# Gate and up projections of experts 3 to 16: half of the K-tiles in three passes of split operands, with weights moved in runs of 4096 bytes

## The chip, the cores and the metric

One core of a Trainium2 chip runs the whole program in one launch. The metric is the time on the device in microseconds (us), median of three runs.

## What is computed

Two layers of a transformer block on 512 tokens of 1024 features, all in float32. A layer is a mixer (three kinds of attention, 12 gated projections) and then a mixture of 16 experts, of which each token takes two. The change touches the experts alone:

```python
hid = jax.nn.silu(jnp.einsum('bsd,edf->bsef', h, w_g)) * jnp.einsum('bsd,edf->bsef', h, w_u)
hid = hid * gate[..., None].astype(hid.dtype)
return jnp.einsum('bsef,efd->bsd', hid, w_d)     # d = 1024, f = 256, 16 experts
```

`h` is the normed input (`rms_norm(x, norm_ffn_g[l])`). An expert's weights are 3 MB: 1 MB each for gate, up and down.

## The kernel before

Each engine has its own program, written out by hand, and the engines meet at semaphores. Nothing is scheduled by a tool: the order of the code is the order on the engine.

**The experts, one after the other.** Expert e has up to 128 token slots. GpSimd gathers their normed rows from DRAM into `gather_rows` (two buffers, `gather_tokens`). TensorE turns them in eight transposes into the banks S[0] and S[1] (`turn_gathered`). ScalarE (S[0]) and VectorE (S[1]) copy them into `et`, times the gain of the norm (`et_out`). TensorE multiplies them by the gate and up weights, 8 K-tiles of 128 rows, side by side in one bank of 512 columns (`gate_up`); these are plain float32 matmuls, and the hardware takes two instructions per K-tile. ScalarE takes silu, VectorE the product with up; TensorE turns the result (`turn_hidden`), VectorE splits it into a high and a low part (`hid_hi`, `hid_lo`), and TensorE multiplies by the down weights in three passes of fp32r operands (`down`, by the helper `three`: high by low, low by high, high by high). ScalarE writes the high part of the down weights (`weights_hi`), GpSimd the low part (`weights_lo`). The rows go out times their weight (`rows_down` on ScalarE for one half, VectorE for the other), and GpSimd adds them into DRAM with an indirect DMA (`add_rows`).

**The order on TensorE** for step e of the loop is: `gate_up(e)`, `turn_gathered(e + 1)`, `down(e - 1)`, `turn_hidden(e)`. In this text T(e) is the moment at which `gate_up(e)` ends. ScalarE then does silu(e), `et_out(e + 1)`, `rows_down(e - 1)`, `weights_hi(e)`. VectorE does the product (e), `et_out(e + 1)`, the second half of the rows (e - 1), `hid_hi` and `hid_lo` (e). GpSimd does gather (e + 3), `weights_lo(e)`, `add_rows(e - 1)`. In steps 1 and 2 VectorE also works out the routing of the tokens past 128 of an expert (`route_rows`, `route_blocks`).

**The weights** lie in a ring `work` of six slots of 1 MB, three pieces per expert: K-tiles 0 to 3 of gate and up (piece 0), K-tiles 4 to 7 (piece 1), down (piece 2). SyncE's queue issues them in order, and a slot is loaded again when its old piece is used up:

```python
used, per = ((first_half, 1), (gu_done, 1), (down_lo, 2))[(n - RING) % PIECES]
sp.wait_ge(used, per * ((n - RING) // PIECES + 1))
```

A K-tile takes rows k x 128 to k x 128 + 127 of the matrix, so a partition gets a run of 256 floats, 1024 bytes, from each K-tile, and 4096 bytes from each row of down.

Semaphores that the change and the prediction touch: `gu_done` (gate_up(e) ended), `first_half` (its first four K-tiles ended), `et_act` and `et_dve` (the two halves of `et` written), `hid_done` (product ready), `down_hi` and `down_lo` (parts of the down weights ready), `piece_in` (a slot loaded), `e_hot`, `e_counted`, `e_known` (routing of the tokens past 128).

Of the kernel before, what the change touches and what calls it, by code (L numbers as in the profile page):

```python
# [60 lines left out]
PIECES = 3  # L61

# [116 lines left out]
def hybrid_block(nc, x, rel_bias, norm_mix_g, w_in, qk_norm_g, diff_lambda, diff_subln_g, sinks, w_branch,  # L179
# [24 lines left out]
    with ctx:  # L204
# [67 lines left out]

        wr = sb("wr", [P, KT, 20])
# [82 lines left out]
        pre_eids = sem("pre_eids")  # L356

# [91 lines left out]
        down_lo = sem("down_lo")  # L449
        down_done = sem("down_done")  # L450
# [19 lines left out]
                     down_lo, down_done, y_act, y_dve, x_stored, w_ready, w_counted, w_known]  # L470
# [60 lines left out]
        def _(sp):  # L531
# [83 lines left out]
            parameters(0)  # L615
            sp.dma_start(probs[0:N_BUCKETS, 1, 0:REL_HEADS], rel_bias).then_inc(pre_b, 16)
# [3 lines left out]
            for l in range(DEPTH):  # L620
# [27 lines left out]
                for n in range(PIECES * N_EXPERTS):  # L648
# [30 lines left out]
                def over_weights(i):  # L679
                    e = sp.value_load(over_expert[0:1, i:i + 1], min_val=0, max_val=N_EXPERTS - 1)  # L680
                    le = l * N_EXPERTS + e
                    for part in range(PIECES):
# [8 lines left out]
                        if part < 2:  # L691
                            for half, w in enumerate((w_ff_gate, w_ff_up)):
                                src = w.rearrange("l e d f -> (l e) d f")[bass.ds(le, 1), part * 512:(part + 1) * 512, :]
                                sp.dma_start(work[:, slot, :, half * FF:(half + 1) * FF],
                                             src.rearrange("a (k p) n -> p (a k) n", p=P)).then_inc(piece_in[slot], 16)
# [14 lines left out]
        def _(pool):  # L710
# [27 lines left out]
            for l in range(DEPTH):  # L738
# [117 lines left out]
        def _(pe):  # L856
# [280 lines left out]
            def gate_up(e):  # L1137
                if e:
                    pe.wait_ge(et_act, e + 1)
                    pe.wait_ge(et_dve, e + 1)  # L1140
                if e >= 2:
                    pe.wait_ge(hid_done, e - 1)
                for part in range(2):
                    n = PIECES * e + part
                    pe.wait_ge(piece_in[n % RING], 32 * (n // RING + 1))
                    for kk in range(4):
# [5 lines left out]
                        if e == 0 and kt == 4:  # L1152
                            pe.wait_ge(et_dve, 1)
                        last = nc.tensor.matmul(G[e % 2][:, :], et[:, e % 2, kt * P:(kt + 1) * P],  # L1154
                                                work[:, n % RING, kk, :], start=(kt == 0), stop=(kt == KT - 1))
# [11 lines left out]
            def down(e):  # L1167
# [4 lines left out]
                for c in range(2):  # L1172
                    if e < N_EXPERTS - 1:
                        pe.wait_ge(down_lo, 2 * e + c + 1)
# [14 lines left out]
            for l in range(DEPTH):  # L1189
# [67 lines left out]
                for e in range(N_EXPERTS + 1):  # L1257
# [19 lines left out]
                    if e == 4:  # L1277
# [8 lines left out]
                    if e == 5:  # L1286
# [1016 lines left out]
```

## Time and profile before

| | |
|---|---|
| time, median of 3 runs | 1417.36 us (1416.01 to 1417.49) |
| span of the profiled execution, first to last instruction | 1414.7 us |
| what lies around the span, from the median | 2.7 us |
| TensorE busy | 1380.1 us (98%) |
| VectorE, ScalarE, GpSimd busy | 747.1, 501.9, 762.0 us |
| experts of layer 0 / layer 1 in the span | about 516 to 699 us / 1220 to 1412 us |

The profile is of one execution. Busy time is a sum over instructions; what a second of an engine is worth is read from the chain of work that ended last. SyncE's rows are DMA issues, not transfers.

### The profile page before, as it was taken

To read this page: it belongs to the slowest core of one execution; us is meant where nothing else is said; L and a number is where in the kernel's file an instruction comes from. 1 tells how busy PE (TensorE), PEld (TensorE's weight loads), DVE (VectorE), ACT (ScalarE), POOL (GpSimd) and SP (SyncE) were. 2 spreads that over 40 slices of the span, in tenths; PEclk is the share of its full clock that TensorE was granted. 3 is DMA by queue.
4 is the path that set the end of the run, shared out by engine and by line. 5 is a ranking of instruction groups with operands and counts; after the bars stand their busy time and mean duration, and the time that the engine had idled before them with its cause. 6 is when DMAs were issued, how large, how long until landed. Compare 5 with 4: busy or idle time off the path is not lost.

```text
span 1414.7 us, 19421 instructions
## 1 busy us (share of the span) xinstructions
PE 1380.1 (98%) x6804; PEld 1014.5 (72%) x6804; DVE 747.1 (53%) x1917; ACT 501.9 (35%) x1194; POOL 762.0 (54%) x643
## 2 busy tenths in 40 slices
PE   7999999999999999999889999999999999999997
PEld 5788877777777866656477887777777778665563
DVE  4487856656684155222146787675658543452221
ACT  4322333433432143334243332334343412343331
POOL 4566654454445625676545575544444554266763
PEclk9999999999999999999899999999999999999999
DMA  5435322223312758999732243222322147689995
GB/s 153 127 101 172 118 79 82 74 70 102 88 61 75 278 198 288 322 348 339 197 115 77 69 121 90 80 63 84 84 95 78 61 143 267 234 272 332 329 345 133
DMA packets 148567, 224.26 MB, mean 159 GB/s; under 512 B 18634, under 2 KB 95876, under 8 KB 148462
## 3 DMA queue, kind: packets, MB, share of 16 engines
q1 hardware_dynamic: 136030, 197.59, 43.4%
q0 software_dynamic: 9936, 16.81, 5.0%
q10 hardware_dynamic: 2496, 8.52, 1.5%
q8 instruction: 58, 0.95, 0.3%
q14 instruction: 47, 0.39, 0.1%
HBM read 215.47 MB, written 31.25 MB: 174 GB/s over the span
## 4 chain that ended last, share of the span: by engine, by line
PE 91%; DVE 4%; ACT 1%; issue 1%; POOL 1%; DMA 1%; SPq 0%; POOLq 0%; DVEq 0%; ACTq 0%
PE bank L859 20%; PE bank L861 18%; PE bank L860 18%; PE bank L1154 16%; PE bank L1035 4%; PE bank L1047 3%; PE bank L1068 2%; PE bank L1116 2%; PE bank L988 1%; PE bank L1058 1%; DVE probs L1849 1%; PE bank L1001 1%; POOL w_lo L733 1%; DVE mixed L1666 1%; PE bank L1126 1%
## 5 line engine op out<-in xcount | busy, mean ns | idle before, releaser
L727 POOL TENSOR_SCALAR w_hi<-raw 128x1024 fp32r<-128x1024 f32 (+2 forms) x142 | 148.7, 1047 | 418.1 <-PE bank L861 415.3
L733 POOL TENSOR_TENSOR w_lo<-raw,w_hi 128x512 fp32r<-128x512 f32 (+2 forms) x288 | 359.1, 1267 | 16.4 <-ACT w_hi L1579 4.6
L860 PE MATMUL bank<-w_hi,hT_lo 128*128 128x512 f32 (+2 forms) x696 | 258.5, 371 | 0.0
L1154 PE MATMUL bank<-work,ptmp 128*128 128x512 f32 x512 | 225.5, 592 | 1.0 <-ACT ptmp L1515 1.0
L859 PE MATMUL bank<-w_lo,hT_hi 128*128 128x512 f32 (+2 forms) x576 | 216.2, 375 | 2.4 <-DVE hT_lo L1674 1.0
L861 PE MATMUL bank<-w_hi,hT_hi 128*128 128x512 f32 (+2 forms) x576 | 211.6, 367 | 0.0
L1154 PEld LDWEIGHTS bank<-work,ptmp 128*128 128x128 f32 x512 | 94.6, 190 | 107.6 <-issue 106.2
L795 POOL TENSOR_TENSOR w_lo<-work,w_hi 128x512 fp32r<-128x512 f32 x120 | 148.1, 1263 | 43.0 <-ACT w_hi L1531 43.0
L859 PE MATMUL bank<-hT_lo,w_hi 128*128 128x512 f32 x384 | 159.5, 415 | 0.0
L861 PE MATMUL bank<-hT_hi,w_hi 128*128 128x512 f32 x384 | 150.7, 393 | 0.0
L860 PE MATMUL bank<-hT_hi,w_lo 128*128 128x512 f32 x384 | 150.1, 391 | 0.0
L860 PEld LDWEIGHTS bank<-w_hi,hT_lo 128*128 128x128 f32 x696 | 131.2, 188 | 20.5 <-issue 0.5
L859 PEld LDWEIGHTS bank<-w_lo,hT_hi 128*128 128x128 f32 x576 | 108.4, 188 | 28.8 <-issue 8.5
L861 PEld LDWEIGHTS bank<-w_hi,hT_hi 128*128 128x128 f32 x576 | 108.4, 188 | 17.8
L859 PEld LDWEIGHTS bank<-hT_lo,w_hi 128*128 128x128 f32 x384 | 72.1, 188 | 32.8 <-issue 20.5
L2118 DVE TENSOR_TENSOR sq<-sq,bank 128x256 f32<-128x256 f32 x32 | 13.4, 420 | 150.8 <-ACT sq L1623 150.8
L861 PEld LDWEIGHTS bank<-hT_hi,w_hi 128*128 128x128 f32 x384 | 72.1, 188 | 16.5
L771 POOL DMA_INDIRECT probs<-normed_dram,slot_token x32 | 33.2, 1037 | 89.9 <-PE bank L1116 67.6
L860 PEld LDWEIGHTS bank<-hT_hi,w_lo 128*128 128x128 f32 x384 | 72.4, 188 | 12.5
L859 PE MATMUL bank<-oT_lo,w_hi 128*128 128x512 f32 x192 | 79.4, 413 | 0.5 <-DVE hT_lo L1907 0.5
L1623 ACT ACTIVATE sq<-bank 128x256 f32<-128x256 f32 x32 | 12.3, 384 | 184.4 <-PE bank L1154 184.4
L861 PE MATMUL bank<-oT_hi,w_hi 128*128 128x512 f32 x192 | 76.1, 396 | 0.0
(308 smaller groups left out, 2342.7 us busy)
## 6 DMA issues: line engine op xcount, KB each, us to landing
work<-in_w_ff_gate SPq DMA_DIRECT2D x66, 512.0 KB
work<-in_w_ff_up SPq DMA_DIRECT2D x66, 512.0 KB
work<-in_w_ff_down SPq DMA_DIRECT2D x33, 1024.0 KB, 6.7
raw<-in_w_gate SPq DMA_DIRECT2D x48, 512.0 KB, 3.9
raw<-in_w_in SPq DMA_DIRECT2D x40, 512.0 KB, 3.5
raw<-in_w_branch SPq DMA_DIRECT2D x24, 512.0 KB, 3.6
raw<-in_w_out SPq DMA_DIRECT2D x16, 512.0 KB, 3.7
normed_dram<-mixed ACTq DMA_DIRECT2D x8, 512.0 KB, 2.7
```

The costliest lines, as they stand in the source:

```text
L727: nc.gpsimd.tensor_scalar(w_hi[:, two, :, 0:w], raw[:, slot, :, 0:w], 1.0, 0.0, ALU.mult, ALU.add).then_inc(split_hi, 1)
L733: last = nc.gpsimd.tensor_tensor(w_lo[:, two, kk, 0:w], raw[:, slot, kk, 0:w], w_hi[:, two, kk, 0:w].bitcast(F32), ALU.subtract)
L771: nc.gpsimd.indirect_dma_start(out=gather_rows[:, e % 2, :], out_offset=None, in_=xn_dram, in_offset=bass.IndirectOffsetOnAxis(ap=rows, ax ...
L795: last = nc.gpsimd.tensor_tensor(w_lo[:, c, f, :], rows[:, f, c * 512:(c + 1) * 512], w_hi[:, c, f, :].bitcast(F32), ALU.subtract)
L859: nc.tensor.matmul(out_ap, s_hi, m_lo, start=start, stop=False)
L860: nc.tensor.matmul(out_ap, s_lo, m_hi, start=False, stop=False)
L861: return nc.tensor.matmul(out_ap, s_hi, m_hi, start=False, stop=stop)
L1035: last = nc.tensor.matmul(S[m][:, cols], q[r, job.u, job.i * P:(job.i + 1) * P], k[r, keys], start=True, stop=True)
L1047: last = nc.tensor.transpose(T[0][:, col:col + P], prob_bufs[job.g % 3][:, mm, b * P:(b + 1) * P], ident[:, :])
L1068: last = nc.tensor.matmul(O[HD * m:HD * (m + 1), job.i * P:(job.i + 1) * P], v, p[:, m, b * P:(b + 1) * P], start=(b == 0), stop=(b == len ...
L1116: last = nc.tensor.transpose(S[a][:, q * P:(q + 1) * P], gather_rows[:, e % 2, dt * P:(dt + 1) * P], ident[:, :])
L1154: last = nc.tensor.matmul(G[e % 2][:, :], et[:, e % 2, kt * P:(kt + 1) * P], work[:, n % RING, kk, :], start=(kt == 0), stop=(kt == KT - 1))
```

## The change

For experts 2 to 15 (the third to the sixteenth; `splits(e)`), in each of the two layers, K-tiles 4 to 7 of `gate_up` are taken in three passes of fp32r parts in place of float32 matmuls. The gathered half in S[1] is copied to `et_hi` by ScalarE without the gain, and VectorE subtracts to get `et_lo`. The gain goes to the weights: ScalarE writes `gu_hi` (weights times gain, four instructions of 128x512), VectorE `gu_lo` (the rest), both two experts ahead of their use. The low part of the second half of the down weights moves from GpSimd to VectorE (`down_lo_half`). K-tile k of gate and up now takes every fourth row of a half of the matrix, so that a partition's four rows are one run of 4096 bytes; the gathered rows are written in the same order of features, and the gains are loaded in it (`ffn_gain`, two small loads at the start). `route_blocks` is cut in two, for steps 2 and 3, and what TensorE, VectorE and the waits do with it comes one step later. Experts 0, 1 and the blocks past 128 tokens keep float32, in the new order.

```diff
+FIRST_SPLIT = 2
+def split_count(e):
+    return 4 * (e - FIRST_SPLIT + 1)
...
+        et_hi, et_lo = hT_hi[:, 0:2, :], hT_hi[:, 2:4, :]
+        gu_hi_bufs = [[oT_hi[:, k, :] for k in range(4)], [hT_lo[:, k, :] for k in range(4)]]
+        gu_lo_bufs = [[oT_lo[:, k, :] for k in range(4)], [hT_hi[:, 5, :], hT_hi[:, 6, :], hT_hi[:, 7, :], hT_lo[:, 6, :]]]
+        def splits(e):
+            return FIRST_SPLIT <= e < N_EXPERTS
+        def in_expert_order(rows):
+            return rows.rearrange("p (a n k) -> p a k n", a=2, k=4)
+        def gate_up_piece(slot):
+            return work[:, slot].rearrange("p k n -> p (k n)").rearrange("p (h k n) -> p h k n", h=2, k=4)
...
+            for m in range(DEPTH):
+                sp.dma_start(ffn_gain[:, m, :].rearrange("p (a k) -> p a k", k=4),
+                             layer_of(norm_ffn_g, m).rearrange("l (a p k) -> p (l a) k", a=2, k=4)
+                             ).then_inc(gains_in, 16)
...
-                        used, per = ((first_half, 1), (gu_done, 1), (down_lo, 2))[(n - RING) % PIECES]
-                        sp.wait_ge(used, per * ((n - RING) // PIECES + 1))
+                        old = (n - RING) // PIECES
+                        if part == 0:
+                            sp.wait_ge(first_half, old + 1)
+                        elif part == 1 and splits(old):
+                            sp.wait_ge(gu_lo, split_count(old))
+                        elif part == 1:
+                            sp.wait_ge(gu_done, old + 1)
+                        else:
+                            sp.wait_ge(down_lo, old + 2)
+                            if old:
+                                sp.wait_ge(down_lo_dve, old)
...
-                            sp.dma_start(work[:, slot, :, half * FF:(half + 1) * FF],
-                                         src.rearrange("a (k p) n -> p (a k) n", p=P)).then_inc(piece_in[slot], 16)
+                            sp.dma_start(gate_up_piece(slot)[:, half],
+                                         src.rearrange("a (p k) n -> p (a k) n", p=P)).then_inc(piece_in[slot], 16)
...
-                    for c in range(2):
+                    for c in range(1 if e else 2):
                         pool.wait_ge(down_hi, 2 * e + c + 1)
...
+                    if part and splits(e):
+                        pe.wait_ge(et_dve, e + 1)
+                        for kk in range(4):
+                            pe.wait_ge(gu_lo, split_count(e - 1) + kk + 1)
+                            rows = slice(kk * P, (kk + 1) * P)
+                            last = three(G[e % 2][:, :], et_hi[:, e % 2, rows], et_lo[:, e % 2, rows],
+                                         gu_hi_bufs[e % 2][kk], gu_lo_bufs[e % 2][kk], False, kk == 3)
+                        last.then_inc(gu_done, 1)
+                        continue
...
+                if splits(e):
+                    act.wait_ge(et_turned, 2 * e + 2)
+                    nc.scalar.activation(et_hi[:, e % 2, :], S[1][:, :], ACT.Copy).then_inc(et_hi_done, 1)
+            def gate_up_hi(e):
+                n = PIECES * e + 1
+                act.wait_ge(piece_in[n % RING], 32 * (n // RING + 1))
+                for kk in range(4):
+                    nc.scalar.activation(gu_hi_bufs[e % 2][kk].rearrange("p (h n) -> p h n", h=2),
+                                         gate_up_piece(n % RING)[:, :, kk, :], ACT.Copy,
+                                         scale=ffn_gain[:, l, 4 + kk:5 + kk]).then_inc(gu_hi, 1)
...
                     if 1 <= e < N_EXPERTS - 1:
                         weights_hi(e)
+                    if splits(e + 2):
+                        gate_up_hi(e + 2)
...
+                if splits(e):
+                    v.wait_ge(et_hi_done, e - FIRST_SPLIT + 1)
+                    nc.vector.tensor_tensor(et_lo[:, e % 2, :], S[1][:, :], et_hi[:, e % 2, :].bitcast(F32),
+                                            ALU.subtract).then_inc(et_dve, 1)
+                    return
...
+            def gate_up_lo(e):
+                n = PIECES * e + 1
+                for kk in range(4):
+                    v.wait_ge(gu_hi, split_count(e - 1) + kk + 1)
+                    nc.vector.scalar_tensor_tensor(gu_lo_bufs[e % 2][kk].rearrange("p (h n) -> p h n", h=2),
+                                                   gate_up_piece(n % RING)[:, :, kk, :], ffn_gain[:, l, 4 + kk:5 + kk],
+                                                   gu_hi_bufs[e % 2][kk].bitcast(F32).rearrange("p (h n) -> p h n", h=2),
+                                                   ALU.mult, ALU.subtract).then_inc(gu_lo, 1)
+            def down_lo_half(e):
+                v.wait_ge(down_hi, 2 * e + 2)
+                nc.vector.tensor_tensor(w_lo[:, 1, :, :], down_rows(e)[:, :, 512:1024], w_hi[:, 1, :, :].bitcast(F32),
+                                        ALU.subtract).then_inc(down_lo_dve, 1)
...
+                    if 1 <= e < N_EXPERTS - 1:
+                        down_lo_half(e)
...
+                    if splits(e + 2):
+                        gate_up_lo(e + 2)
+                    if e in (2, 3):
+                        route_blocks(e - 2)
```

On TensorE, from the end of step 1 to step 2 of layer 0, before: the turn of the hidden rows (`sq`), `gate_up` (`work` by `ptmp`, where `et` lies), the turn of the gathered rows (`probs`), and the first K-tile of `down`:

```order
L1163 MATMUL bank<-ident,sq 128x128 x2
L1154 MATMUL bank<-work,ptmp 128x512 x8
L1116 MATMUL bank<-ident,probs 128x128 x8
L859 MATMUL bank<-w_lo,hT_lo 128x512
L860 MATMUL bank<-w_hi,hT_lo 128x512
L861 MATMUL bank<-w_hi,hT_lo 128x512
```

The same place in the changed kernel (`gu_hi` and `gu_lo` of an even expert lie in `oT_hi` and `oT_lo`):

```order
L1215 MATMUL bank<-ident,sq 128x128 x2
L1205 MATMUL bank<-work,ptmp 128x512 x4
L900 MATMUL bank<-oT_lo,hT_hi 128x512
L901 MATMUL bank<-oT_hi,hT_hi 128x512
L902 MATMUL bank<-oT_hi,hT_hi 128x512
...
L1157 MATMUL bank<-ident,probs 128x128 x8
L900 MATMUL bank<-w_lo,hT_lo 128x512
```

Four of the eight K-tiles stay float32, and the other four are three matmuls each (12 rows, of which three are shown).

On ScalarE, one step before: silu, `et_out`, `rows_down`, `weights_hi`, and the silu of the next step:

```order
L1623 ACTIVATE sq<-bank 128x256
L1515 ACTIVATE ptmp<-bank,pcol 128x128 x4
L1540 ACTIVATE mixed<-bank,slot_weight 128x512
L1531 ACTIVATE w_hi<-work 128x1024 x2
L1623 ACTIVATE sq<-bank 128x256
```

And of the change, where `gu_hi` lies in `oT_hi` or in `hT_lo`:

```order
L1693 ACTIVATE sq<-bank 128x256
L1570 ACTIVATE ptmp<-bank,ffn_gain 128x128 x4
L1581 ACTIVATE hT_hi<-bank 128x512
L1607 ACTIVATE mixed<-bank,slot_weight 128x512
L1598 ACTIVATE w_hi<-work 128x1024 x2
L1588 ACTIVATE oT_hi<-work,ffn_gain 128x512 x4
L1693 ACTIVATE sq<-bank 128x256
```

Five instructions per step are new: `et_hi` (L1581), which stands ahead of `rows_down`, and the four of `gate_up_hi` (L1588), which stand ahead of the next silu.

On VectorE, step 2 of the change: product, `et_lo`, rows, `hid_hi`, `hid_lo`, then what is new, `down_lo_half` (L2200), `gate_up_lo` (L2192) and the first half of `route_blocks` (L2161 on), and the product of step 3:

```order
L2215 TENSOR_TENSOR sq<-sq,bank 128x256
L2179 TENSOR_TENSOR hT_hi<-bank,hT_hi 128x512
L2225 TENSOR_SCALAR mixed<-bank,slot_weight 128x512
L2235 CAST hT_lo<-bank 128x256
L2237 TENSOR_TENSOR hT_lo<-bank,hT_lo 128x256
L2200 TENSOR_TENSOR w_lo<-work,w_hi 128x1024
L2192 SCALAR_TENSOR_TENSOR oT_lo<-work,ffn_gain,oT_hi 128x512 x4
L2161 SCALAR_TENSOR_TENSOR raw<-raw,rank 128x8
L2164 TENSOR_SCALAR raw<-o_rows,raw 128x128 x4
...
L2215 TENSOR_TENSOR sq<-sq,bank 128x256
```

The product of the next step, on which TensorE's next `turn_hidden` waits, now stands behind `gate_up_lo`.

## Rows read from the trace of the kernel before

**Rows 1.** The page's slices: granted clock and DMA share, each over 1/40 span.

```profile
PEclk9999999999999999999899999999999999999999
DMA  5435322223312758999732243222322147689995
```

**Rows 2.** The chain that ended last, one expert: start us, us, what.

```profile
608.22 6.87 PE bank L1154 x16
615.08 0.87 PE bank L1116 x8
615.96 0.23 PE bank L859
...
618.49 0.23 PE bank L861
618.72 0.22 PE bank L1163 x2
618.93 6.44 PE bank L1154 x15
```

**Rows 3.** Timeline of the other engines, one expert: start us, us, engine, line.

```profile
604.41 0.38 ACT L1623 ACTIVATE sq<-bank 128x256 f32<-128x256 f32 x1 [5.88 <-PE bank L1154]
604.84 1.14 ACT L1515 ACTIVATE ptmp<-bank,pcol 128x128 f32<-128x128 f32 x4
...
606.67 0.69 ACT L1540 ACTIVATE mixed<-bank,slot_weight 128x512 f32<-128x512 f32 x1 [0.69 <-PE bank L861]
607.26 1.99 ACT L1531 ACTIVATE w_hi<-work 128x1024 fp32r<-128x1024 f32 x2
...
608.39 4.94 POOL L795 TENSOR_TENSOR w_lo<-work,w_hi 128x512 fp32r<-128x512 f32 x4 [1.35 <-ACT w_hi L1531]
...
609.15 0.42 DVE L2140 TENSOR_TENSOR hT_lo<-bank,hT_lo 128x256 fp32r<-128x256 f32 x1
...
613.36 0.37 SPq L667 DMA_DIRECT2D work<-in_w_ff_down  x1
```

**Rows 4.** DMA from 576 to 684 us: share in 40 slices, queues.

```profile
DMA  9999997999999999999999999999999999999998
...
DMA packets 26245, 36.20 MB, mean 335 GB/s; under 512 B 2470, under 2 KB 22406, under 8 KB 26239
...
q1 hardware_dynamic: 23301, 30.89, 83.4%
q0 software_dynamic: 2938, 5.22, 19.5%
```

**Rows 5.** Queue q1, 668 to 670 us, then 594 to 596: packets, MB, share.

```profile
q1 hardware_dynamic: 661, 0.72, 111.9%
...
q1 hardware_dynamic: 195, 0.80, 99.7%
```

**Rows 6.** Groups by form: busy us, mean ns, idle before.

```profile
L1504 ACT ACTIVATE hT_hi<-bank 128x512 fp32r<-128x512 f32 x16 | 9.6, 600 | 39.1 <-DVE bank L1903 39.1
...
L1611 ACT ACTIVATE mixed<-X,row_rs 128x1024 f32<-128x1024 f32 x8 | 9.2, 1152 | 2.7 <-ACT mixed L1611 2.5
...
L1579 ACT ACTIVATE w_hi<-raw 128x512 fp32r<-128x512 f32 x4 | 2.3, 623 | 8.0 <-PE bank L861 8.0
...
L1907 DVE SCALAR_TENSOR_TENSOR hT_lo<-bank,hT_hi 128x512 fp32r<-128x512 f32 x16 | 11.0, 686 | 0.3
```

**Rows 7.** Timeline, steps 1 and 2: GpSimd, VectorE and the SyncE queue.

```profile
542.33 4.94 POOL L795 TENSOR_TENSOR w_lo<-work,w_hi 128x512 fp32r<-128x512 f32 x4 [1.38 <-ACT w_hi L1531]
...
543.66 2.40 DVE L2066 SCALAR_TENSOR_TENSOR raw<-rank,raw 128x8 f32<-128x8 f32 x2
...
547.29 0.37 SPq L667 DMA_DIRECT2D work<-in_w_ff_down  x1
...
554.38 3.89 DVE L2082 TENSOR_SCALAR raw<-o_rows,raw 128x128 f32<-128x128 f32 x4
...
558.29 0.97 DVE L2082 TENSOR_SCALAR raw<-o_rows,raw 128x128 f32<-128x128 f32 x4
```

More of the change, by code:

```diff
@@ L356, in hybrid_block @@
         pre_eids = sem("pre_eids")
+        gains_in = sem("gains_in")
         par = sem("par")
@@ L693, in over_weights @@
                                 src = w.rearrange("l e d f -> (l e) d f")[bass.ds(le, 1), part * 512:(part + 1) * 512, :]
-                                sp.dma_start(work[:, slot, :, half * FF:(half + 1) * FF],
-                                             src.rearrange("a (k p) n -> p (a k) n", p=P)).then_inc(piece_in[slot], 16)
+                                sp.dma_start(gate_up_piece(slot)[:, half],
+                                             src.rearrange("a (p k) n -> p (a k) n", p=P)).then_inc(piece_in[slot], 16)
                         else:
@@ L1139, in gate_up @@
                     pe.wait_ge(et_act, e + 1)
+                if e and not splits(e):
                     pe.wait_ge(et_dve, e + 1)
@@ L1154, in gate_up @@
                         last = nc.tensor.matmul(G[e % 2][:, :], et[:, e % 2, kt * P:(kt + 1) * P],
-                                                work[:, n % RING, kk, :], start=(kt == 0), stop=(kt == KT - 1))
+                                                gate_up_piece(n % RING)[:, :, kk, :], start=(kt == 0),
+                                                stop=(kt == KT - 1))
                     last.then_inc(first_half if part == 0 else gu_done, 1)
@@ L1172, in down @@
                 for c in range(2):
-                    if e < N_EXPERTS - 1:
-                        pe.wait_ge(down_lo, 2 * e + c + 1)
+                    if e < N_EXPERTS - 1 and (c == 0 or e == 0):
+                        pe.wait_ge(down_lo, e + 2 if e else c + 1)
+                    elif e < N_EXPERTS - 1:
+                        pe.wait_ge(down_lo_dve, e)
                     if e >= 1:
@@ L1311, in over_block @@
                             last = nc.tensor.matmul(G[0][:, :], et[:, 0, kt * P:(kt + 1) * P],
-                                                    work[:, n % RING, kk, :], start=(kt == 0), stop=(kt == KT - 1))
+                                                    gate_up_piece(n % RING)[:, :, kk, :], start=(kt == 0),
+                                                    stop=(kt == KT - 1))
                     last.then_inc(e_gu, 1)
@@ L2074, in route_rows, with route_blocks @@
                 link(nc.vector.tensor_reduce(listed, a_cmp[:, :, :, :], AX.X, ALU.add))
-            def route_blocks():
-                block, later, listed = (a_calc[:, n] for n in range(3))
+            def route_blocks(half):
+                block, later, listed, late_weight = (a_calc[:, n] for n in range(4))
+                for t in range(TT) if half else ():
+                    nc.vector.tensor_scalar(over_onehot[:, 1, t, :], slot_id, block_rank[:, 1, t:t + 1], None,
+                                            ALU.is_equal)
+                if half:
+                    for k in range(2):
+                        link(nc.vector.tensor_tensor(over_token[:, k, :, 8:16], over_token[:, k, :, 0:8],
+                                                     late_weight[:, k].unsqueeze(2).broadcast_to([P, TT, 8]), ALU.mult))
+                        last = nc.vector.tensor_tensor(over_token[:, k, :, 0:8], over_token[:, k, :, 0:8],
+                                                       later[:, k].unsqueeze(2).broadcast_to([P, TT, 8]), ALU.mult)
+                    last.then_inc(e_hot, 1)
+                    return
@@ L2078, in route_blocks @@
                 link(nc.vector.scalar_tensor_tensor(block_rank[:, :, :], block, -float(CAPACITY), rank[:, :, :],
                                                     ALU.mult, ALU.add))
+                for t in range(TT):
+                    nc.vector.tensor_scalar(over_onehot[:, 0, t, :], slot_id, block_rank[:, 0, t:t + 1], None,
+                                            ALU.is_equal)
                 for k in range(2):
-                    for t in range(TT):
-                        nc.vector.tensor_scalar(over_onehot[:, k, t, :], slot_id, block_rank[:, k, t:t + 1], None,
-                                                ALU.is_equal)
@@ L2087, in route_blocks @@
                 link(nc.vector.scalar_tensor_tensor(later, block, 0.5, tokens[:, :].unsqueeze(1).broadcast_to([P, 2, TT]),
                                                     ALU.is_gt, ALU.mult))
-                late_weight = a_calc[:, 3]
                 link(nc.vector.scalar_tensor_tensor(late_weight, block, 0.5, weight[:, :, :], ALU.is_gt, ALU.mult))
-                for k in range(2):
-                    link(nc.vector.tensor_tensor(over_token[:, k, :, 8:16], over_token[:, k, :, 0:8],
-                                                 late_weight[:, k].unsqueeze(2).broadcast_to([P, TT, 8]), ALU.mult))
-                    last = nc.vector.tensor_tensor(over_token[:, k, :, 0:8], over_token[:, k, :, 0:8],
-                                                   later[:, k].unsqueeze(2).broadcast_to([P, TT, 8]), ALU.mult)
@@ L2096, in route_blocks @@
-                last.then_inc(e_hot, 1)
             def et_out(e):
```

35 lines of the change are left out of this document (21 added, 14 removed).

## The prediction

> **What bounds the kernel now.** I read the table of busy times first: TensorE is busy 98% of the span, every other engine about half. The slices show its clock at full rate almost throughout, and the DMA line standing out in two stretches, 6 to 10 tenths against 2 to 4 elsewhere: those are the experts [rows 1]. Then the chain of work that ended last, through one expert. It is TensorE without a gap: `gate_up` 6.87 us, eight transposes 0.87, twelve three-pass matmuls of `down` (one each 0.23) and two transposes to 618.93, so 10.71 us from one `gate_up` to the next [rows 2]. Third, the timeline of the others in such a period. With T the end of `gate_up` (604.37, one period before 615.08), silu starts at T+0.04, the four copies of `et` end at T+1.6, `weights_hi` ends at T+4.9, VectorE's `hid_lo` at T+5.2, GpSimd's `weights_lo` at T+9.0, and SyncE's queue sends the next pieces at T+9.0 [rows 3]. None holds TensorE. Last the DMA: from 576 to 684 us no slice is under 7 tenths, the two queues together are at 103% (packets in flight overlap), and 36.20 MB in 108 us are 3.59 MB per expert [rows 4]. So two resources are full: TensorE, on the chain, and the DMA, not on it, but with no room.
>
> **TensorE's part.** A float32 K-tile costs 6.87/8 = 0.859 us, and there are four of them: 3.435. A three-pass K-tile costs what one of `down` costs: (618.72 - 615.96)/4 = 0.69, four are 2.76, entry from the transposes included [rows 2]. Saved: 0.675 an expert, which I round to 0.67 for switching kinds of operand inside a bank, a step that no row shows alone. 14 experts x 2 layers x 0.67 = **18.8 us**. The period becomes 10.05. Below this, 0.58 would be 16.2 in all, if the switch costs the 0.09 that separates the first pass from the others at its worst. The clock, already at the 2.4 GHz level, can't add anything [rows 1].
>
> **ScalarE's part.** `et_hi`, a plain copy from a bank, is priced 0.60 [rows 6]. The four of `gate_up_hi` read SBUF: 0.62 without a scale, and a scale from SBUF adds a tenth (1.15 for 1024 columns with it, about 1.05 as in 1.99 for two without [rows 3, 6]); back to back I take 0.65 each, 2.6. ScalarE's 4.2 of 10.7 become 7.4 of 10.05: it is no bound. But its place in the order matters. `gate_up_hi(e+2)` stands ahead of silu(e+1) and waits for piece 1 of expert e+2, which before was needed only by TensorE almost a period later. How late may it be? From silu's start to the end of `et` are 1.6 us, and `gate_up` starts 3.85 after T (618.93 - 615.08) [rows 2, 3]. So silu may start at T+2.3, and with 2.6 of its own work ahead of it the piece must have landed by **T(e+1) - 0.3**.
>
> **VectorE's part.** Per step `down_lo_half` (1024 columns; 0.686 for 512, so about 1.2) and four of `gate_up_lo` (0.69 each, 2.75) [rows 6]. With the old 2.7 it is 6.7 of 10.05. There is a hold-up: while GpSimd worked on `w_lo` without a break, two VectorE instructions on 8 columns of SBUF took 2.40 us, each waiting for a GpSimd instruction (4.94/4 = 1.24) to end; four of 128 columns took 3.89 against 0.97 for four when GpSimd was done [rows 7]. Now `down_lo_half` at T+5.2 meets GpSimd's two instructions (T+4.0 to T+6.5, then a little later), and `gate_up_lo` begins about T+7.7 and ends near T+10.3, the next product being due at T+10.05+0.45. It just fits. The Trainium skill (GPSIMD Engine Reference, Key points) says the same: GpSimd shares its SBUF interfaces with VectorE, in contention with instructions of two SBUF inputs. By that rule each of the five new VectorE instructions can be held; the trace agrees in 1.2 us a time.
>
> In steps 1 to 3 VectorE also has `route_rows` and the halves of `route_blocks` (four at 0.97 and a handful of 0.2: 2.1 us) behind `gate_up_lo`, ahead of the product [rows 7]. In step 2 `gate_up_lo(4)` can't end before the first long burst has landed (557, below) and 2.6 + 0.65 more: 560; the blocks end at 562.2, the product of step 3 at 562.6, while TensorE wants it at T(3)+3.6 = 562.0. So 0.5 to 1 us is lost here, and perhaps 0.3 in step 3. I take **1 us a layer**, 0 to 2.
>
> GpSimd loses two instructions of 1.24 per expert and gains nothing; the moved routing has a whole step of room; the two gain loads go out in the first 20 us, where TensorE waits for norms. The scaled copies to DRAM stay 1.15 each before TensorE's first expert, now with strided input. All of this: 0, up to +1.
>
> **The DMA's part.** Same bytes, but two of three pieces in packets of 4096 in place of 1024 bytes. Piece 2 already has such packets. A stretch of 661 packets (mean 1.09 KB) moved 0.72 MB in 2 us, one of 195 packets (4.1 KB) 0.80 MB [rows 5]. For 2.10 MB: 5.83 against 5.25 us, **0.58 less** an expert. Since the engines had no gaps I set the DMA's work for an expert at the period, 10.72, so W = 10.14 after; uncertain by 0.3. The Trainium skill (DMA: Bandwidth & Descriptors, Why small descriptors are slow) gives about 3 cycles per packet on top of one per 32 bytes: 35/32 against 131/128, 6.4% less, 0.37 us of 5.83, W = 10.35. The same page puts HBM to SBUF at about 358 GB/s per core, which would make W 3.59/0.358 = 10.03; the row of 0.80 MB in 2 us is above that limit, so I don't use it.
>
> Is it in time? The first steady burst went out at 547.29, behind `weights_lo(1)` [rows 7]. GpSimd now has half (542.33 + 2.5), so 544.8. With 10.14 of transfer and 2 for issue and landing (my allowance) piece 1 of expert 4 lands at 557. The k-th lands at 557 + (k-1)W, and is needed by T(k+2) - 0.3, where T(2) = 549.0 - 0.67 = 548.3, plus 10.05 a step, plus 1.7 from step 5 for the routing matmuls, plus the 1 us lost above. For the last, k = 12: needed by 671.3, landed at 557 + 11W. So **W up to 10.39 costs nothing**, and what is beyond costs 11 x (W - 10.39) a layer. With 10.14 there is nothing; over the range of W I allow 0.3 a layer.
>
> **The sum.** -18.8 + 2 x 1.0 + 2 x 0.3 = -16.2, and +0.3 for the start: -15.9. The profiled execution has a span of 1414.7, 2.7 under the median, so a span of 1398.8 and a time of **1401.5 us**.
>
> **Rivals.**
> - *The DMA becomes the bound* because 4096-byte runs gain little (the 8% between the two rows is from two short stretches, and the shares beside them, 112% and 100%, could be read as more or less). With W = 10.72, 11 x 0.33 = 3.6 a layer: 1401.5 + 7.3 - 0.6 = 1408. With W = 10.9, since the queue was slipping a little already, 5.6 a layer: 1412. For it: the unbroken nines. Against: what is in flight at 103% may not be the limit. Chance 0.27, 1405 to 1413.
> - *Everything hides*: the burst lands by 556, VectorE gets ahead of GpSimd, no loss in steps 2 and 3: 1417.4 - 18.8 = 1398.5. Chance 0.14.
> - *Slower*: larger packets of the weights push the indirect queue aside (gather and scatter share the 16 engines, 19.5% [rows 4]), silu waits for piece 1 in each step, and W rises instead. All gain is gone when 11 x (W - 10.39) = 8, at W = 11.1; at 11.5 it is 12.2 a layer and 1425. The Trainium skill (DMA: Bandwidth & Descriptors, Queues, rings and completion order) says that an engine changes between queues only at a packet's end, which is the mechanism; the trace holds no case of it, both kinds of packet having stood beside the indirect queue in each period. Chance 0.06.
> - *The change buys nothing on TensorE*, a three-pass tile costing what a float32 one does when operands switch: within 0.2% of before. `down` shows 0.69 in the same loop. Chance 0.03.
>
> **The numbers.** Likeliest, 1399.5 to 1405: 0.50. The range 1398 to 1411 takes in most of the first two rivals and leaves some 0.17 out. A difference of 0.2% (2.8 us) is about what a measurement of this kernel tells from none. Faster: 0.50 + 0.14 + 0.26 = 0.90; same 0.04; slower 0.06.
>
> **What would show it.** In the new trace: periods of 10.05 on the chain, `gate_up`'s second half at 2.76; `gate_up_hi` starting at T+7.5 to T+9, its wait put down to the DMA or to nothing; gaps on TensorE only ahead of `turn_hidden` in steps 2 to 4, released by VectorE's product. If instead TensorE waits for `et` (ScalarE) in late steps, and more with each, the DMA is the bound. Wrong altogether: a period over 10.4 from the first steps on.

## The result, and the profile after

Slower: **1434.87 us** (median of 4 runs, 1433.97 to 1438.44) against 1416.93 (4 runs, 1416.01 to 1417.49) on the same chip, a ratio of 1.0133 with the interval [1.0118, 1.0147]. The prediction was 1401.5. The span of the profiled execution is 1433.6, 18.9 more than before.

The DMA share in the slices of the changed kernel's page, to be held against [rows 1]:

```profile
DMA  5436322222213758999632242322322246688894
```

The end of the DMA line, layer 1's experts, reads 46688894 where it read 47689995. The queues in layer 0, 576 to 684 us, which answers to [rows 4]:

```profile
DMA  9969993799999998999189979998899879998999
...
DMA packets 10896, 35.05 MB, mean 325 GB/s; under 512 B 2355, under 2 KB 2355, under 8 KB 10890
...
q1 hardware_dynamic: 8062, 29.89, 73.1%
q0 software_dynamic: 2828, 5.08, 18.7%
```

The share of q1 is 10 points lower, and there are holes in a line that had none under 7. The share has to be read with care: runs_only, below, has 76.0% without a single late step, so most of the fall is the longer packets. What is left is 29.89 MB in the 108 us against 30.89: fewer bytes, and yet the weights are late. The page's line of the chain that ended last, by engine:

```profile
PE 78%; DMA 8%; DVE 5%; ACT 3%; issue 3%; POOL 3%; SPq 1%; ACTq 0%; POOLq 0%; DVEq 0%
```

The chain through experts 7 and 8 of layer 0, whose answer before is the unbroken TensorE of [rows 2]. Columns: start, us, what.

```profile
601.68 2.28 POOL w_lo L836
...
603.98 0.38 SPq L708
...
605.86 13.48 DMA work<-in_w_ff_up
...
619.36 0.73 ACT hT_lo L1588
...
620.12 1.87 DVE hT_hi L2192 x3
...
622.11 0.74 DVE hT_lo L2192
622.86 0.34 DVE sq L2215
...
623.24 0.65 PE bank L1215 x2
623.89 4.92 PE bank L1205 x8
628.81 0.23 PE bank L900
```

GpSimd's `weights_lo`, the SyncE queue, a transfer, `gate_up_hi` (L1588), `gate_up_lo` (L2192), the product (L2215), and only then `turn_hidden` (L1215). The wait also lets TensorE's clock fall. TensorE does nothing from 620.68 to 623.24, the granted clock is 1.00 up to there, 0.50 (the 1.2 GHz level) from 624 to 626, and 0.87 on the mean from 616.00 to 628.80. The first half of `gate_up` behind the wait takes 4.92 us, against 3.44 at the 2.4 GHz level. Over the whole program TensorE is busy 1376.2 us here, and 1365.1 in queue_order below with the same instructions, so some 11 us of matmul time go with the loss. They are not on the loop described below: from 562 to 690 us no silu waits for TensorE. What waits from 520 to 720 us (engine, line and what it waits for; total, times, longest):

```profile
POOL w_lo L836 <- ACT w_hi L1598: 46.6, 14, 5.7
...
ACT oT_hi L1588 <- DMA work<-in_w_ff_up: 34.6, 7, 6.1
...
ACT hT_lo L1588 <- DMA work<-in_w_ff_up: 23.4, 5, 6.0
...
PE bank L1215 <- DVE sq L2215: 11.7, 8, 2.7
```

ScalarE waits 58 us for piece 1 in twelve steps, and that comes back as VectorE's and GpSimd's waits for ScalarE.

**Where the 18.9 us went.** I took the start of silu in each step as the mark of a step. Three lengths make up the whole difference:

| us | before | after |
|---|---|---|
| first silu of layer 0 | 527.6 | 529.7 (+2.0) |
| its 15 steps | 162.5 | 169.4 (+6.9) |
| last silu of layer 0 to first of layer 1 | 535.3 | 538.6 (+3.4) |
| the 15 steps of layer 1 | 162.5 | 169.1 (+6.6) |

The steps of layer 0 are 8.7, 11.8, 12.0, 12.2, 12.9, 9.8, 12.0, 12.8, 10.2, 11.3, 11.5, 11.5, 13.0, 10.4, 9.4. Without a wait (queue_order, below) the first is 8.7, the second and the sixth, with the routing matmuls, 11.8, and the others are the 10.05 of the prediction. So the loops cost 13.5 us in place of saving 18.8, a loss of 32, and the stretches ahead of them 5.4 more.

### The profile page after: what moved, and what is told of

The parts are those of the page before. It is cut to its first block, busy times and chain, and to the rows that moved or that the text cites. A ratio compares the mean times of both kernels' runs of the same rounds, so it can differ in the third digit from the quotient of the medians.

```text
span 1433.6 us, 19905 instructions
## 1 busy us (share of the span) xinstructions
PE 1376.2 (96%) x6916; PEld 1038.3 (72%) x6916; DVE 850.1 (59%) x2057; ACT 587.8 (41%) x1334; POOL 723.5 (50%) x587
## 4 chain that ended last, share of the span: by engine, by line
PE 78%; DMA 8%; DVE 5%; ACT 3%; issue 3%; POOL 3%; SPq 1%; ACTq 0%; POOLq 0%; DVEq 0%
PE bank L900 19%; PE bank L902 18%; PE bank L901 18%; DMA work<-in_w_ff_up 6%; PE bank L1205 5%; PE bank L1076 4%; PE bank L1088 3%; PE bank L1109 2%; PE bank L1029 1%; PE bank L1099 1%; ACT mixed L1679 1%; POOL w_lo L836 1%; PE bank L1157 1%; SPq L705 1%; PE bank L1042 1%
## 5 line engine op out<-in xcount | busy, mean ns | idle before, releaser
L836 POOL TENSOR_TENSOR w_lo<-work,w_hi 128x512 fp32r<-128x512 f32 x64 | 103.7, 1639 | 87.8 <-ACT w_hi L1598 87.7
L1205 PE MATMUL bank<-work,ptmp 128*128 128x512 f32 x288 | 138.8, 629 | 0.7 <-ACT ptmp L1570 0.7
L902 PEld LDWEIGHTS bank<-w_hi,hT_hi 128*128 128x128 f32 x576 | 108.5, 188 | 17.8
L1205 PEld LDWEIGHTS bank<-work,ptmp 128*128 128x128 f32 x288 | 55.6, 203 | 59.7 <-issue 58.6
L900 PEld LDWEIGHTS bank<-hT_lo,w_hi 128*128 128x128 f32 x384 | 72.1, 188 | 32.9 <-issue 20.5
L901 PE MATMUL bank<-oT_hi,w_lo 128*128 128x512 f32 x192 | 75.7, 394 | 0.0
L1501 ACT ACTIVATE probs<-probs,job_neg 128x256 f32<-128x256 f32 (+5 forms) x128 | 66.5, 523 | 14.5 <-DVE job_neg L1904 14.4
```

Of the source, the lines that this page charges most:

```text
L836: last = nc.gpsimd.tensor_tensor(w_lo[:, c, f, :], rows[:, f, c * 512:(c + 1) * 512], w_hi[:, c, f, :].bitcast(F32), ALU.subtract)
L900: nc.tensor.matmul(out_ap, s_hi, m_lo, start=start, stop=False)
L901: nc.tensor.matmul(out_ap, s_lo, m_hi, start=False, stop=False)
L902: return nc.tensor.matmul(out_ap, s_hi, m_hi, start=False, stop=stop)
L1501: last = nc.scalar.activation(p, p, ACT.Exp, bias=job_neg[:, g % 4, m:m + 1], scale=-1.0, accum_out=job_sum[:, g % 4, m:m + 1])
```

## The experiments

**Theory A, a loop of latency.** The queue sends a burst for each expert: down(e), then pieces 0 and 1 of e+1. It sends it only when `weights_lo(e-2)` is done, because down(e) stands first. That work comes after `gate_up_hi(e-1)` on ScalarE, which waits for piece 1 of e-1, from the burst two before. So a landing releases the issue of a later burst. In the chain above, from the issue of one burst (603.98) to that of the burst it releases: 15.4 to the landing (619.36), 2.5 to silu (621.82), 2.3 to `w_hi` (624.14), 1.2 to `w_lo`, 3.5 for it, and the burst leaves at 628.80. That is 24.8 us for two experts. By A, the cure is to send piece 1 without waiting for `w_lo`. The other bursts of layer 0 agree: behind each of the eleven landings from 559.66 to 676.69 (the start of `gate_up_hi`, which waits for the piece) the burst two further on leaves after 9.4 to 9.6 us, every time.

**Rival B, throughput:** the DMA engines need some 11.5 us for an expert's weights, whatever the order. **Rival C, compute:** VectorE's longer list, with `gate_up_lo` ahead of the product and VectorE and GpSimd holding each other up in the low parts, would cost the time even with weights at hand. **Rival D, the packets:** the long runs themselves disturb the transfers.

The first four ran beside the kernel before at 1416.37 us (16 runs). First the two halves of the change.

**runs_only**, the runs of 4096 bytes without the split:

```diff
-            return FIRST_SPLIT <= e < N_EXPERTS
+            return False
# and both halves of w_lo on GpSimd, as before
```

> The changed kernel with no expert split: all K-tiles of gate and up in float32 and both halves of the low part of the down weights on GpSimd, as before; what stays is the 4096-byte layout, the strided copy of the normed rows and the gain loads. Both theories: TensorE sets the step (10.72 us), so the layout can't gain there, and the strided copies (2.13 against 1.15 us, four ahead of each layer's first expert) cost what the changed kernel shows at the start of the experts, 2.0 us in layer 0 and 3.4 in layer 1. Expected 1422, and steps of 10.7 us. If the layout harmed the transfers, steps would be longer than 10.72.

Measured 1420.82 us, ratio 1.003 [1.0018, 1.0041]. The steps are 10.71 to 10.72 and the loops as long as before (162.2, 162.5); the 5.7 us of its span lie in the two starts, +2.0 and +4.0. Its queues, 576 to 684 us:

```profile
q1 hardware_dynamic: 8353, 30.95, 76.0%
q0 software_dynamic: 2903, 5.26, 19.5%
```

The same bytes as [rows 4] in 7 points less of the engines' time, but not in less time: 335 GB/s before and 336 here, since TensorE sets the pace. The long runs buy nothing here, where the DMA held nothing up, and cost at the start. Rival D is out.

**split_only**, the split with the old layout:

```diff
-   src.rearrange("a (p k) n -> p (a k) n", p=P)
+   src.rearrange("a (k p) n -> p (a k) n", p=P)
# plain copy of X to xn, gains from pcol
```

> The changed kernel with the 1024-byte layout of before (K-tiles of 128 neighbouring rows, plain copy of the normed rows, gain from the old column tile). Theory A (loop of latency: each burst of three pieces is sent only after GpSimd and VectorE have finished weights that stand behind the landing of an earlier burst; a burst takes 12 us from first issue to landing): a burst takes 0.5 us longer, so a step grows from 11.5 to 11.8 or 12.1, 28 steps, +8 to +17, and the start gives 5.4 back: 1438 to 1446. Rival B (the DMA engines' throughput is the limit and 4096-byte runs gave nothing): 1429.5, the start alone. A value above 1434 speaks for the runs helping.

Measured 1439.49 us, 1.0157 [1.0138, 1.0176]. Its loops take 171.9 and 173.1, its first silu is back at 527.8. The loss is in the split; the long runs soften it, since the changed kernel's loops are 2.5 and 4.0 us shorter (one profiled execution of each). It is inside A's range and 10 us above B's figure. The share of q1 from 576 to 684 us is 82.0%, with the weights as late as in the changed kernel: a high share doesn't rule out such a loop.

**queue_order**: the changed kernel, and piece 1 sent ahead of the down weights that wait for `w_lo`:

```diff
-                for n in range(PIECES * N_EXPERTS):
+                order = list(range(11))
+                for e in range(4, N_EXPERTS):
+                    order += [PIECES * e + 1, PIECES * e - 1, PIECES * e]
+                for n in order + [PIECES * N_EXPERTS - 1]:
```

> The changed kernel with one edit in SyncE's order: from expert 4 on, piece 1 of an expert is issued ahead of the down piece of the expert before and of its own piece 0. Same bytes, same packets. Theory A: piece 1's slot is free a whole step before it is now asked for, so it lands about a step earlier, ScalarE no longer waits and TensorE runs at 10.05 us a step: 32 us come back, 1403 to 1408. Rival B (throughput): the same bytes take the same time, steps stay at 11.5 and the time within 3 us of 1434.9. Rival C (VectorE held by GpSimd sets the step): also unchanged.

Measured **1405.07 us** (1402.43 to 1405.51), 0.9913 [0.9897, 0.993]. No instruction of any compute engine differs from the changed kernel, only the order of the DMA issues, and 29.8 us are back. The chain from 606 us:

```profile
606.36 3.44 PE bank L1208 x8
609.80 0.23 PE bank L903
...
612.36 0.23 PE bank L905
612.59 0.87 PE bank L1160 x8
...
616.22 0.22 PE bank L1218 x2
616.44 1.72 PE bank L1208 x4
```

TensorE without a gap, 10.08 us a period, with `gate_up`'s second half in 612.59 - 609.80 = 2.79. SyncE's queue in this kernel:

```profile
600.43 0.47 SPq L708 DMA_DIRECT2D work<-in_w_ff_gate  x1
600.94 0.43 SPq L708 DMA_DIRECT2D work<-in_w_ff_up  x1
602.54 0.33 SPq L708 DMA_DIRECT2D work<-in_w_ff_gate  x1
602.91 0.48 SPq L708 DMA_DIRECT2D work<-in_w_ff_up  x1
610.07 0.38 SPq L711 DMA_DIRECT2D work<-in_w_ff_down  x1
```

Piece 1 (602.54) leaves 7.5 us ahead of the down weights (610.07), behind which it used to stand. The loops take 153.0 and 153.4, 32 less than in the changed kernel and together 18.6 less than before: the 18.8 of the prediction. The stretches ahead of them, 530.0 and 539.9, cost 7.0 in this execution, so 11.6 of the 18.6 are left. A holds. B is out: the same bytes in the same packets now go in steps of 10.06. C can't be the cause, since its instructions are all still there.

**one_ahead**: the parts of gate and up made one expert ahead, behind `et_out`, not two:

```diff
+                        if splits(e + 1):
+                            gate_up_hi(e + 1)      # behind et_out(e + 1); gate_up_lo likewise
...
-                    if splits(e + 2):
-                        gate_up_hi(e + 2)          # at the end of step e
```

> The changed kernel with ScalarE's and VectorE's split of piece 1 moved: for expert e+1 behind the copies of the gathered rows in step e, in place of expert e+2 at the end of step e. The piece is asked for about 7.3 us later. SyncE's order as in the changed kernel. Theory A: the wait of ScalarE (3 to 6 us a step) falls inside those 7.3 us, steps near 10.05 to 10.3: 1404 to 1412. Rival B (throughput, 11.5 us of DMA work per expert): only a head start of 7.3 us a layer is won, 1420. Rival C (VectorE's work does not fit in a step): no gain, 1430 or more, since the order only moves.

Measured 1420.01 us (10 runs, 1415.15 to 1426.97, the widest spread of all), 1.0027 [1.001, 1.0043]: 15 us won, but outside what A gave. It is B's figure, so this run by itself speaks for B, which only queue_order refutes. Its waits from 520 to 720 us:

```profile
POOL w_lo L836 <- DVE mixed L2227: 43.3, 10, 5.5
...
ACT oT_hi L1588 <- DMA work<-in_w_ff_up: 12.8, 5, 3.2
```

(The code has GpSimd wait for ScalarE's `w_hi` in the first line; it and VectorE's `mixed` end within 0.1 us of each other.) The new place puts `gate_up_hi` ahead of `rows_down` and `weights_hi`: `w_hi` starts 5.7 us behind silu (608.27 - 602.56), not 2.3, so `w_lo` and the burst behind it come later too. Part of the slack goes back into the loop. I had not counted this in A's number. Some steps are at 10.05, and those that wait do so for the DMA.

The next four ran beside 1416.75 us (9 runs).

**pool_lo**: both halves of `w_lo` back on GpSimd, the queue as in the changed kernel.

```diff
-                    for c in range(1 if e else 2):
+                    for c in range(2):
...
-                    if 1 <= e < N_EXPERTS - 1:
-                        down_lo_half(e)
```

> The changed kernel with both halves of the low part of the down weights on GpSimd as before, SyncE's order unchanged. Rival C (VectorE's instructions with two SBUF inputs and GpSimd hold each other up, w_lo takes 3.5 us in place of 2.5): taking one of them away from VectorE shortens the step, time under 1430. Theory A: what counts is when the last of the low parts is done, since SyncE's queue waits for it: four instructions of 1.24 in place of 3.5 us, 1.5 us later per burst, half of it in each step of the two-step loop: 1440 to 1455.

Measured 1447.84 us, 1.0221 [1.0206, 1.0237]. One step of its timeline:

```profile
603.53 4.99 POOL L834 TENSOR_TENSOR w_lo<-work,w_hi 128x512 fp32r<-128x512 f32 x4 [1.42 <-ACT w_hi L1594]
608.54 0.38 SPq L706 DMA_DIRECT2D work<-in_w_ff_down  x1
```

`w_lo` takes 4.99 in place of 3.50, and the burst leaves 0.02 us behind it. With 1.5 us more in a loop of two experts, 28 steps would lose 28 x 0.75 = 21; 13 are lost. So moving half of `w_lo` to VectorE helps here, and C, which had the time fall under 1430, is refuted. The hold-up is real all the same, and it is in the loop: 3.50 us where two instructions alone take 2.5.

**down_last**: piece 0, piece 1, then down, another order that takes piece 1 out from behind `w_lo`.

```diff
+                    order += [PIECES * e, PIECES * e + 1, PIECES * e - 1]
```

> The changed kernel with SyncE's order of each burst turned: piece 0, piece 1, then the down piece, whose wait for the low parts of the down weights is no longer ahead of the others. Piece 1 goes first or second in its burst in place of last, so it lands about a third of a burst, 3 us, earlier, and is sent a little earlier. Theory A: ScalarE's wait falls from 3 to 6 us to 0 to 3, most of the loss goes: 1408 to 1420. If only a whole step of lead helps (queue_order), it stays near 1430.

Measured 1408.99 us, 0.9944 [0.9929, 0.9959]. Nearly as good as queue_order, but piece 1 now waits for piece 0's slot, and ScalarE still waits for it:

```profile
ACT oT_hi L1591 <- DMA work<-in_w_ff_up: 22.7, 7, 4.8
ACT hT_lo L1591 <- DMA work<-in_w_ff_up: 18.7, 6, 4.0
```

**order_and_turn**: queue_order, but ScalarE copies the rows plainly and TensorE's transposes read every fourth column.

```diff
-    gather_rows[:, e % 2, dt * P:(dt + 1) * P], ident[:, :])
+    in_expert_order(gather_rows[:, e % 2, :])[:, a, q, :], ident[:, :])
```

> queue_order with the normed rows copied to DRAM in plain order (ScalarE reads without stride, 1.15 us each as before), the stride of four floats taken by TensorE's loads in the turn of the gathered rows in place of it. If the start loss is ScalarE's strided read, 4 x 1 us ahead of the gather less what the routing covers, 2.0 us in layer 0 and 2.0 to 3.4 in layer 1 come back: 1399.5 to 1401. If TensorE's strided loads cost too, the eight transposes go from 0.87 to as much as 1.7 us in each of 33 steps and eat 0 to 27 us.

Measured 1409.06 us, 0.9947 [0.9933, 0.996], slower than queue_order by 4: the loops take 154.8 each, 3.3 more together, and at the starts nothing is gained. The stride costs more on TensorE, as the groups by form from 500 to 560 us show, first of this kernel, where `mixed` is read with the stride:

```profile
L1170 PE MATMUL bank<-ytmp,mixed 128*128 128x128 f32 x32 | 7.7, 399 | 0.1
...
L1160 PE MATMUL bank<-ident,probs 128*128 128x128 f32 x24 | 3.5, 288 | 0.0
```

and then of queue_order, where it is read plainly:

```profile
L1170 PE MATMUL bank<-ytmp,mixed 128*128 128x128 f32 x32 | 3.8, 277 | 0.1
L1160 PE MATMUL bank<-ident,probs 128*128 128x128 f32 x24 | 3.2, 275 | 0.0
```

The first group, 3.9 us longer, stands ahead of each layer's first expert and eats what ScalarE's plain copies save.

**order_short_runs**: queue_order with the old layout, that is both edits of queue_order and split_only.

> queue_order with the 1024-byte layout of before (and its plain copy of the normed rows and old gain tile). Measures what the 4096-byte runs are worth once nothing else holds the DMA. Where the transfer work is 10.7 us an expert with short packets, as I read the trace of before, steps grow from 10.05 to near 10.6 after the slack of the ring is used up, 4 to 7 us a layer, less 5 for the start: 1405 to 1412. If short packets are as fast, the time is 1400, the start alone. If they are slower than I took them, above 1412.

Measured **1400.42 us** (4 runs, 1398.31 to 1400.86), 0.9879 [0.9863, 0.9894], the best version of all: 1.2% faster than the kernel before. The stretches ahead of its two loops are 2.6 and 2.7 us shorter than those of queue_order, and its loops take 154.0 and 153.4. So with the order mended the long runs are worth 1.0 us in layer 0 and nothing in layer 1, and cost about 5 at the starts. Its queues, 576 to 684 us:

```profile
q1 hardware_dynamic: 25449, 30.51, 82.8%
q0 software_dynamic: 2811, 5.12, 19.4%
```

The DMA line is as full as before the change, and still TensorE loses a microsecond only. That is the "short packets are as fast" of the expectation, and it refutes how I had read the trace of before, as 10.7 us of transfer work an expert with no room. From 560 to 660 us this kernel moves 348 GB/s and queue_order 353, where the kernel before moved 338; from 1270 to 1370 us they move 345 and 344, against 335. At 3.59 MB an expert that is an estimate of 10.2 to 10.4 us with either kind of packet, so the next bound is near: in layer 0 ScalarE waits 0.3 to 2.9 us for piece 1 in five steps from 625.75 us on, in layer 1 up to 1.5 in three.

The last two ran beside 1417.57 us (7 runs), to see if more is to be had on top of order_short_runs. **order_short_pool** adds pool_lo's edit, **order_short_late** that of one_ahead.

> order_short_runs with both halves of the low part of the down weights on GpSimd, as before the change. In the changed kernel this move cost 13 us, which theory A puts down to the later issue of the next burst. Theory A: with piece 1 ahead of the down piece the wait is no longer in the way, and GpSimd has the time (two more instructions of 1.24 in a step of 10.05), so 1400 to 1402. If GpSimd's or VectorE's own time set the step, as rival C has it, it would be 1410 or more.

> order_short_runs with the split of piece 1 one expert ahead in place of two (the move of one_ahead). In order_short_runs layer 0 still loses 0.9 us in its last steps to pieces that land late with short packets. Theory A: with the order of the queue right, either place of the split meets its piece in time; the later place has 7 us more for the landing but puts the high and low parts of the down weights 2.6 us later, which the down piece's issue waits for: 1399.5 to 1402, no worse than order_short_runs. If the later low parts hold up the down piece and with it piece 0 behind it, steps grow again: above 1405.

Measured 1402.22 us, 0.9892 [0.9876, 0.9909], and 1401.78 us, 0.9897 [0.9881, 0.9914]. The intervals overlap that of order_short_runs: neither edit does anything that can be told apart, once the loop is cut (the first is 0.2 us above its range, the second inside). The same two had moved the time by +13 and -15 us while it was closed.

## Why the prediction was wrong

**The step that failed** is in the DMA's part: "The k-th lands at 557 + (k-1)W". It takes the bursts as one transfer after another without a pause, so that only the rate counts. That was so before, when nothing that the queue waited for hung on a recent landing: piece 1 was wanted by TensorE alone, most of a period later. The change puts `gate_up_hi` on ScalarE ahead of silu and `weights_hi`, and so a landing ahead of the release of the queue's next burst. I had seen the wait ("its place in the order matters") and worked out how late the piece may land, but had not followed what a late piece does to the next issue. The rate was near enough: 10.14 us an expert in the prediction, and an estimate of 10.2 from queue_order's 353 GB/s. In the changed kernel, a burst that met a nearly empty queue,

```profile
628.80 0.38 SPq L708 DMA_DIRECT2D work<-in_w_ff_down  x1
...
630.97 0.47 SPq L705 DMA_DIRECT2D work<-in_w_ff_up  x1
```

landed at 640.79, 12.0 us later, the 10.14 + 2 of the prediction. That the queue was nearly empty is in the DMA view of 628 to 630 us (packets, MB, share):

```profile
q1 hardware_dynamic: 19, 0.06, 13.4%
```

With 12.0 to the landing and 9.4 from there to the next issue (24.8 - 15.4) the loop is 21.4 us for two experts, so 10.7 for one, even if no burst stands behind another. That is an estimate from these rows, and it is the sum I should have made: it alone takes the whole gain of 10.72 - 10.05. Over the eleven bursts from 547.57 to 661.73 the landing came after 12.0 to 15.5 us, 13.6 on the mean; with the 9.5 from there to the issue, half of it is 11.55, the mean interval of the bursts from 547.57 to 686.14. The extra over 12.0 goes with overlap: the two that left within 0.7 us of the landing before them needed 12.0 and 12.3, those that left 1.7 to 3.4 ahead of it 13.0 to 15.5 (the one at 603.98, the one before it having landed at 606.51, 15.4). No run separates the two by itself.

**The first burst** was late too. "GpSimd now has half (542.33 + 2.5)": the first long burst left at 547.57, not 544.8.

```profile
544.04 3.50 POOL L836 TENSOR_TENSOR w_lo<-work,w_hi 128x512 fp32r<-128x512 f32 x2 [1.37 <-ACT w_hi L1598]
545.14 1.25 DVE L2200 TENSOR_TENSOR w_lo<-work,w_hi 128x1024 fp32r<-128x1024 f32 x1
547.57 0.38 SPq L708 DMA_DIRECT2D work<-in_w_ff_down  x1
```

`w_lo` took 3.50, not 2.5: I had let VectorE be held by GpSimd [rows 7], and not GpSimd by VectorE. It also started 1.7 later, but so did the step itself (silu at 538.34 for 536.62), which is the lost start below and no delay against TensorE. The first landing was at 559.66 for 557, the second at 571.85 for 567.1.

**The start**, the other term mis-sized, was put at +0.3 and cost 5.4. "The scaled copies to DRAM stay 1.15 each … now with strided input": they don't. The group by form of the changed kernel, 500 to 520 us, to [rows 6]:

```profile
L1679 ACT ACTIVATE mixed<-X,row_rs 128x1024 f32<-128x1024 f32 x4 | 8.5, 2133 | 1.3 <-ACT mixed L1679 1.2
```

0.98 more each, four in a row ahead of the gather, and in place of a chain over TensorE stands one over these copies, the write to DRAM and the gather. In layer 1 TensorE then waits 2.16 us for the gathered rows and works behind the wait at a granted clock of 0.75: the first expert's twelve matmuls take 6.85 in place of 5.15.

**What was right.** TensorE's part: 0.67 an expert; queue_order's loops gained 18.6 of the 18.8. The prices of the new ScalarE and VectorE instructions, within 0.1 us: 2.56 for four of `gate_up_hi` (2.6), 0.61 for `et_hi` (0.60), 748 ns each for `gate_up_lo` (690); only `down_lo_half` came to 1.5 (1.2). That VectorE's list fits: in queue_order the steps behind the first are 10.05 to 10.08, or 11.8 with the routing matmuls.

**What was right by luck.** W = 10.14 came out near, but not by the way it was worked out. The 10.72 for short packets was TensorE's period and not the DMA's work: order_short_runs moves the same packets in steps of 10.05. And the 0.58 that long runs were to save doesn't show as time: 353 against 348 GB/s in layer 0, 344 against 345 in layer 1, and 1.0 us of the loops. What fell in runs_only is the share, by 7.4 points of 83.4, which counts packets in flight that overlap. By the Trainium skill (DMA: Bandwidth & Descriptors, Why small descriptors are slow) I had worked out 6.4% for the weights of gate and up alone, so an estimate of 3.5% of an expert; these rates show 1.4% in layer 0 and nothing in layer 1.

**The rivals.** "The DMA becomes the bound" was the nearest, but in the wrong form: queue_order moves the same bytes in steps of 10.06, so what held the changed kernel was the wait between bursts, not the rate. "Slower" had a place for weights that come late in every step, with another mechanism, the indirect queue pushed aside, at 0.06. q0's share from 576 to 684 us is 17.8 to 20.5% in all kernels here, against 19.5% before, and the weights come in time in queue_order with the same long packets. The sign that I named for "wrong altogether", a period over 10.4 from the first steps on, is what the trace showed: 12.0 and 12.2 in the third and fourth steps of layer 0.

**What stays open.** In order_short_runs the stretch from layer 0's last silu to layer 1's first is 2.0 us longer than before (537.25 against 535.26), with the same copies and the same 5.15 us at TensorE's first expert. The traces show where it goes. From ScalarE's first instruction on the new `X` to the table load that follows are 13.8 us (701.42 to 715.26) against 10.9 before (710.72 to 721.66), and the granted clock of the first 11 of them is 0.57 against 0.88. order_short_late, with the same copies, takes 535.5 for the whole stretch. Why the clock stays low there, and whether it does so in each execution, no run shows.

## What to carry to other kernels

When an edit makes an engine wait for a transfer earlier than before, don't ask only whether the transfer's rate suffices: follow that wait through the engine's list to what it releases, and see whether a later DMA issue is among it. If so, the period is at least the time round that loop (issue, latency, transfer, everything queued on the way) over the number of buffers it spans. The mark of such a loop is in the times and not in the queue's share (76.0% here without a loop, 73.1 and 82.0 with one): the reader waits for nearly every landing, and each issue leaves a fixed time after an earlier landing. In this kernel the order of issues in the queue was the cheapest place to cut it. Nor is a DMA line full of nines a proof that the DMA has no room: such a line stood beside 338 GB/s and beside 353.

## What the runs showed of the hardware

- ScalarE reading 1024 float32 of SBUF at a stride of four elements: 2133 ns against 1152 without a stride.
- TensorE, float32 operand at the same stride: 399 ns a matmul of 128x128 against 277; the eight transposes of an expert, 288 against 275.
- Two of GpSimd's `w_lo` instructions take 3.50 us beside one of VectorE (1.22 to 2.30 us, median 1.46), against 4.94/4 x 2 = 2.47 alone [rows 3]; the hold-up goes both ways. From 540 to 690 us they average 1688 ns against 1263.
- TensorE, after 2.56 us without work (620.68 to 623.24 in the changed kernel): granted clock 0.50 from 624 to 626, and eight matmuls of 128x512 in 4.92 us against 3.44.
- Packets of 4096 bytes in place of 1024, with the order of issues mended: 353 against 348 GB/s in layer 0, 344 against 345 in layer 1, though the queue's share is 77% against 83%.
- The order of five DMA issues in one queue, with not an instruction changed elsewhere, was worth 30 us of 1435.
